# Mixture-of-experts stage of a two-block model: the smallest group's experts two at a time in plain fp32

## What is computed

```python
def moe_ffn(x, w_router, router_bias, w_gate, w_up, w_down):     # 256 tokens, D = 1024
    scores = jax.nn.sigmoid(jnp.dot(xt, w_router))
    biased = (scores + router_bias).reshape(N, N_GROUPS, EXPERTS_PER_GROUP)   # 4 groups of 4 experts
    group_score = jnp.sum(lax.top_k(biased, TOP_K)[0], axis=-1)
    g_sel = jnp.argmax(group_score, axis=-1)                     # each token picks ONE group
    ...                                                          # and two experts of it
    h = jax.nn.silu(jnp.einsum('nd,edf->enf', xt, w_gate)) * jnp.einsum('nd,edf->enf', xt, w_up)
    h = h * gates.T[:, :, None]                                  # 16 experts, hidden width 256
    y = jnp.einsum('enf,efd->nd', h, w_down)
```

## Time and profile before

| what | value |
|---|---|
| median of 3 runs | 1137.94 us (1137.85 to 1139.21) |
| time of the profiled execution | 1140.78 us |
| its span | 1138.8 us |
| granted TensorE clock | 0.995 of full speed |
| TensorE matmul busy | 1109.2 us, 97% |
| VectorE busy | 796.6 us, 70% |
| ScalarE busy | 587.5 us, 52% |
| HBM read | 212.63 MB |

### The profile page before, as it was taken

The page is one execution under the profiler, slowest core; times in us unless marked ns, Lnnn a source line. Parts: engine busy times, 40 slices in busy tenths (PEclk is TensorE's granted clock), DMA queues, the critical chain, the costliest instruction groups (busy, mean ns, idle before and its releaser), DMA issues.

```text
span 1138.8 us, 17173 instructions
## 1 busy us (share of the span) xinstructions
PE 1109.2 (97%) x6740; PEld 968.9 (85%) x6740; DVE 796.6 (70%) x1012; ACT 587.5 (52%) x744; POOL 109.1 (10%) x191
## 2 busy tenths in 40 slices
PE   9999999999999999999999999999899999999996
PEld 8999989999788888899787888878797878887885
DVE  5445634687576666659868668996779777578986
ACT  5344455664544344455733456775247624457761
POOL 3000020100000000046300000000156000000000
PEclk9999999999999999999899999999999999999999
DMA  9764444555365555534113969995334119789960
GB/s 297 225 182 126 131 142 147 152 184 182 101 235 184 184 187 192 173 121 149 38 58 105 333 229 322 348 367 199 103 112 148 38 40 294 260 268 350 361 240 38
DMA packets 164983, 214.72 MB, mean 189 GB/s; under 512 B 9778, under 2 KB 145098, under 8 KB 164912
## 3 DMA queue, kind: packets, MB, share of 16 engines
q1 hardware_dynamic: 162288, 209.37, 56.2%
q0 software_dynamic: 1312, 3.88, 1.1%
q10 hardware_dynamic: 1312, 0.49, 0.2%
HBM read 212.63 MB, written 1.09 MB: 188 GB/s over the span
## 4 chain that ended last, share of the span: by engine, by line
PE 84%; DVE 11%; ACT 3%; issue 2%; POOL 0%; ACTq 0%; DVEq 0%
PE ps L863 18%; PE ps L864 18%; PE ps L865 18%; PE ps L1002 7%; PE ps L1001 3%; PE ps L966 3%; PE ps L901 2%; PE ps L899 2%; PE ps L900 2%; DVE wlo L1923 2%; PE ps L940 2%; PE ps L932 2%; PE ps L951 2%; DVE arena L2269 1%; PE ps L924 1%
## 5 line engine op out<-in xcount | busy, mean ns | idle before, releaser
L1923 DVE TENSOR_TENSOR wlo<-raw,whi 128x2048 fp32r<-128x2048 f32 (+3 forms) x157 | 337.6, 2155 | 152.6 <-ACT whi L1531 150.9
L1531 ACT ACTIVATE whi<-raw 128x2048 fp32r<-128x2048 f32 (+3 forms) x157 | 280.9, 1794 | 123.5 <-PE ps L1002 61.5
L863 PE MATMUL ps<-whi,act_both 128*128 128x256 f32 (+2 forms) x464 | 146.2, 315 | 2.8 <-DVE act_both L1940 2.5
L864 PE MATMUL ps<-wlo,act_both 128*128 128x256 f32 (+2 forms) x464 | 144.8, 312 | 0.0
L865 PE MATMUL ps<-whi,act_both 128*128 128x256 f32 (+2 forms) x464 | 144.7, 312 | 0.0
L1923 DVE TENSOR_TENSOR wlo<-arena,whi 128x2048 fp32r<-128x2048 f32 (+1 forms) x48 | 107.9, 2248 | 35.1 <-ACT whi L1531 33.8
L1002 PE MATMUL ps<-act_both,whi 128*128 128x512 f32 x344 | 119.1, 396 | 0.6 <-DVE wlo L1923 0.6
L863 PE MATMUL ps<-act_both,whi 128*128 128x256 f32 x408 | 117.4, 288 | 0.0
L865 PE MATMUL ps<-act_both,wlo 128*128 128x256 f32 x408 | 115.4, 283 | 0.0
L864 PE MATMUL ps<-act_both,whi 128*128 128x256 f32 x408 | 115.4, 283 | 0.0
L1531 ACT ACTIVATE whi<-arena 128x2048 fp32r<-128x2048 f32 (+1 forms) x48 | 90.4, 1884 | 26.5 <-PE ps L865 26.5
(11 more groups left out here) (311 smaller groups left out, 2134.8 us busy)
## 6 DMA issues: line engine op xcount, KB each, us to landing
raw<-in_w_in SPq DMA_DIRECT2D x45, 1024.0 KB, 5.5
raw<-in_w_down SPq DMA_DIRECT2D x27, 1024.0 KB, 5.4
raw<-in_w_gu SPq DMA_DIRECT2D x22, 1024.0 KB, 5.1
arena<-in_w_gate SPq DMA_DIRECT2D x32, 512.0 KB, 5.5
arena<-in_w_up SPq DMA_DIRECT2D x32, 512.0 KB, 7.0
raw<-in_w_gate SPq DMA_DIRECT2D x28, 512.0 KB, 5.2
raw<-in_w_up SPq DMA_DIRECT2D x28, 512.0 KB, 6.6
arena<-in_w_down SPq DMA_DIRECT2D x14, 1024.0 KB, 6.0
```

The source lines that it names most:

```text
L863: pe.matmul(o, ah, bh, start=first, stop=False)
L864: pe.matmul(o, ah, bl, start=False, stop=False)
L1531: act.activation(whi[:, c % 3, 0:n], raw_of(c, v)[:, 0:n], ACT.Copy).then_inc(hi_made, 1)
L1923: dve.tensor_tensor(wlo[:, c % 3, 0:n], raw_of(c, v)[:, 0:n], whi[:, c % 3, 0:n].bitcast(F32), ALU.subtract)\
```

## The change

1. The groups are ranked by size (a VectorE sort of size and number, L2540 to L2548 of the new file). The largest is wide as before, the second and third have 128 slots each, the smallest has 64.
2. The smallest group's four experts leave `MOE_SEQ` and the split rings. They run as two pairs in plain fp32 on the raw tiles. The 64 rows are the stationary operand, once for each half of the array's columns, and expert b of the pair writes PSUM partitions 64b to 64b+63. Tiles P (gate and up of both experts, two blocks of D, 1 MB, four per pair) and Q (down, one half of D, 1 MB, two per pair) hold four matmuls of 512 columns each. They use the same ring of six slots, which they free when TensorE has used them (`pair_used`).
3. P tiles stand behind A4, D1, B4, A5, D2, B5, A6, B6; Q tiles behind D8, B10, D9, B11. The hidden rows of a pair are transposed once for both experts (`turn_pair`).
4. `GU_BANKS` has two banks instead of three; the third is the pairs'.
5. The loops of ScalarE and VectorE go by tile number n: what follows tile n-3 on TensorE is done around the split of tile n. The gather writes 320 columns instead of 384.

```diff
-MOE_SEQ = [0, 1, 2, 4, 5, 6, 7, 8, 9, 10, 11, 12, 13, 14, 15, 3]
+MOE_SEQ = [0, 1, 2, 4, 5, 6, 7, 8, 9, 10, 11, 3]
-GU_BANKS = (0, 1, 3)
+GU_BANKS = (0, 1)
+PAIR_BANK = 3
+PAIR_IN_AFTER = {("A", 4): (0, 0), ("D", 1): (0, 1), ("B", 4): (0, 2), ("A", 5): (0, 3),
+                 ("D", 2): (1, 0), ("B", 5): (1, 1), ("A", 6): (1, 2), ("B", 6): (1, 3)}
+PAIR_OUT_AFTER = {("D", 8): (0, 0), ("B", 10): (0, 1), ("D", 9): (1, 0), ("B", 11): (1, 1)}
+PAIR_TURN_AT = (4, 6)
...
+            def room(i):
+                pair, n = raw_user(i)
+                if pair:
+                    sp.wait_ge(pair_used, n + 1)
+                elif n >= 0:
+                    sp.wait_ge(hi_made, n + 1)
+                    sp.wait_ge(lo_made, n + 1)
...
+                def pair_in(x, i):
+                    n = pair_tile(l, "P", x, i)
+                    room(PAIR_AT[n])
+                    for b in range(2):
+                        for j, w in enumerate(w_gate_up):
+                            d = raw_pair(n)[:, (2 * b + j) * 512:(2 * b + j + 1) * 512].rearrange("p (k c) -> p k c", k=2)
+                            sp.dma_start(d, w[row(12 + 2 * x + b)][:, 2 * i:2 * i + 2, :]).then_inc(raw_in[pair_slot(n)], 16)
...
-                            if kind == "A" and part == 0 and j >= 3:
-                                pe.wait_ge(m_prod, l * 20 + j - 2)
-                            o = ps[:, GU_BANKS[j % 3], :].rearrange("p (a b) -> p a b", a=2)
+                            if kind == "A" and part == 0 and j >= 2:
+                                pe.wait_ge(m_prod, l * 16 + j - 1)
+                            o = ps[:, GU_BANKS[j % 2], :].rearrange("p (a b) -> p a b", a=2)
...
+                def pair_gate_up(x, i):
+                    n = pair_tile(l, "P", x, i)
+                    pe.wait_ge(raw_in[pair_slot(n)], landed_at(PAIR_AT[n]))
+                    if x and i == 0:
+                        pe.wait_ge(pair_prod, l * 2 + x)
+                    w = raw_pair(n).rearrange("p (e two k c) -> p e two k c", e=2, two=2, k=2)
+                    for kk in range(2):
+                        k = 2 * i + kk
+                        for b in range(2):
+                            z = pe.matmul(ps[64 * b:64 * b + 64, PAIR_BANK, :].rearrange("p (a c) -> p a c", a=2),
+                                          xg_pairs[:, k, :], w[:, b, :, kk, :], start=k == 0, stop=k == KD - 1)
+                    z.then_inc(pair_used, 1)
...
                 def gathered(k):
                     dve.wait_ge(xg_h, l * KD + k + 1)
-                    dve.tensor_tensor(xg_lo[:, k, :], ps[:, k, 0:SLOTS], xg_hi[:, k, :].bitcast(F32), ALU.subtract).then_inc(xg_l, 1)
+                    dve.tensor_copy(xg_pairs[:, k, :], ps[:, k, 2 * P:2 * P + 64])
+                    dve.tensor_tensor(xg_lo[:, k, 0:2 * P], ps[:, k, 0:2 * P], xg_hi[:, k, 0:2 * P].bitcast(F32), ALU.subtract).then_inc(xg_l, 1)
...
-                split("A", MOE_SEQ[1])
-                for p in range(1, N_EXP):
-                    product(p - 1)
-                    split("B", MOE_SEQ[p])
...
+                for n in range(FIRST_LOOP, len(MOE_ORDER) + 3):
+                    kind, e, part = MOE_ORDER[n - 3]
+                    if kind == "B" and part == parts_of("B", e) - 1:
+                        product(MOE_SEQ.index(e))
+                    if n < len(MOE_ORDER):
+                        split_lo(T_L + l * L_TILES + J_MOE + n, 0, TW // parts_of(*MOE_ORDER[n][0:2]))
```

More of the change, by code:

```diff
@@ L91, in run_ends, with split_tiles @@
 def run_ends(p):
[L93 to L106, removed]
+    return p == N_RUN - 1 or run_begins(p + 1)
+FLUSH = [p for p in range(N_RUN - 1) if wide(MOE_SEQ[p]) and run_ends(p)]
+GROUP_END = [p for p in range(N_RUN) if not wide(MOE_SEQ[p]) and run_ends(p)]
+PUT_READ = min(p for p in range(N_RUN) if MOE_SEQ[p] // 4 == 2)
 def moe_order():
-    at = {}
+    order, turned, paired, pair_in = [], {}, {}, {}
+    def split_tiles():
+        return sum(kind in "ABD" for kind, e, part in order)
     def add(kind, e):
-        for part in range(parts_of(kind, e)):
-            at[kind, e, part] = len(at)
-    for p in range(N_EXP):
+        order.extend((kind, e, part) for part in range(parts_of(kind, e)))
+        if (kind, e) in PAIR_IN_AFTER:
+            order.append(("P",) + PAIR_IN_AFTER[kind, e])
+            if order[-1][2] == 3:
+                pair_in[split_tiles() - 1] = order[-1][1]
+        if (kind, e) in PAIR_OUT_AFTER:
+            order.append(("Q",) + PAIR_OUT_AFTER[kind, e])
+    for p in range(N_RUN):
         add("A", MOE_SEQ[p])
@@ L137, in moe_used, with pair_tile, raw_sequence, add @@
     return moe_tile(l, kind, e, parts_of(kind, e) - 1) + 1
-def moe_at(n):
-    return (n - T_L) % L_TILES - J_MOE if n >= T_L else -1
+def pair_tile(l, kind, x, i):
+    return l * len(PAIR_ORDER) + PAIR_ORDER.index((kind, x, i))
+def raw_sequence():
+    at, pair_at = {}, {}
+    seq = []
+    def add(slot, transfers, table, n):
+        table[n] = len(seq)
+        seq.append((slot, transfers, table is pair_at, n))
+    for n in range(T_L):
+        add(n % 3, 1, at, n)
+    for l in range(LAYERS):
+        for j in range(J_MOE):
+            n = T_L + l * L_TILES + j
+            add(n % 3, 1, at, n)
+        for i, (kind, e, part) in enumerate(RAW_ORDER):
+            if kind in "PQ":
+                add(i % RAW, 4 if kind == "P" else 2, pair_at, pair_tile(l, kind, e, part))
+            else:
+                add(i % RAW, 1 if kind == "D" else 2, at, moe_tile(l, kind, e, part))
+    return seq, at, pair_at
+J_UQ, J_UKV, J_WO, J_RT, J_MOE = 6, 8, 10, 14, 15
+RAW_SEQ, RAW_AT, PAIR_AT = raw_sequence()
+def landed_at(i):
+    return 16 * sum(transfers for slot, transfers, pair, n in RAW_SEQ[:i + 1] if slot == RAW_SEQ[i][0])
+def raw_user(i):
+    users = [entry for entry in RAW_SEQ[:i] if entry[0] == RAW_SEQ[i][0]]
+    return users[-1][2:] if users else (False, -1)
 def raw_slot(n):
-    return moe_at(n) % RAW if moe_at(n) >= 0 else n % 3
+    return RAW_SEQ[RAW_AT[n]][0]
 def landed(n):
[L152 to L162, removed]
+    return landed_at(RAW_AT[n])
+def pair_slot(n):
+    return RAW_SEQ[PAIR_AT[n]][0]
 L_COLS = [4, 5, 6, 7, 0, 1, 2, 3]
@@ L213, in shape_constants @@
     c[:, C_UP:C_UP + P] = np.arange(P)[:, None] < np.arange(P)[None, :]
[L214 removed]
+    slot = np.arange(SLOTS)
+    c[:, C_SLOT:C_SLOT + SLOTS] = S + np.where(slot < 2 * P + 64, slot, slot - 64)
     dist = S - 1 - np.arange(2 * S)
@@ L1445, in down @@
                             pair = q if wide(e) else GROUP_BANK[e // 4 - 1]
-                            if first and part == 0:
-                                bank_free(p, pair)
+                            if first and part == 0 and not wide(e):
+                                bank_flushed(pair)
                             for half in range(part, 2 // parts + part):
@@ L1455, in down, with scatter @@
                         x.then_inc(tile_used, 1)
-                def scatter(t, half, q0, q1):
-                    for q in range(q0, q1):
+                def scatter(t, half, groups):
+                    for q in groups:
                             w = put_t[:, q, t * P:(t + 1) * P]
```

269 lines of the change are left out of this document (169 added, 100 removed).

## The result

The changed kernel takes 1145.3 us (median of five runs, 1143.39 to 1149.48) against 1137.94: 1.0067 times as long, 95% interval 1.0051 to 1.0082. It is slower; the forecast was 1127 and the range ended at 1143. The profiled execution took 1149.48 us, 8.7 more than the profiled one of before; it is the slowest of the five, so what its trace shows is a little worse than the median.

A forecast was written before the change was run, and what follows sets the result against it. TensorE, its matmuls busy 97% of the span, was taken as the bound. Terms of -34.3 + 24.4 + 0.4 - 0.5 + 3.2 + 1.2 gave -5.6 us a layer, -11.2 for two: 1127 us, range 1116 to 1143.

The forecast's parts named there:

- the pair transposes: Two more pairs of transposes on TensorE cost 0.4 us a layer; the pair's Silu, product and copy cost nothing.
- the term of the transfers: Same 48 MB in less time, queue held back from B8 on; 1.2 us a layer lost by A3.
- a sign of being wrong: The prediction is wrong if the queue, held by `pair_used`, starves TensorE already between A6 and B8.
- the landing time of 1 MB: A 1 MB transfer lands 6.3 us after its issue, 5.2 us where the queue runs dry.
- the 1.2 us at A3: Late weights and a product behind D10's split delay A3; 1.2 us a layer lost.
- the price of a column half: In pair tiles, 512-column passes of 0.43 us run side by side in two halves; 2.03 us a tile.
- rivals 2 and 3: Column halves overlap only in part: about 1138 us, chance 0.13; or don't run side by side: 1166 us, chance 0.14.
- The two banks' wait: A1 waits for expert 0's first product, starting at 642.9 instead of 639.69; 3.2 us a layer lost.
- The gather: 32 matmuls 320 instead of 384 columns wide, two small VectorE operations more; together -0.5 us a layer.
- Rival 4: Transfers become the bound: rate falls to 345 GB/s, some 30 tiles cost 4.5 us a layer; 1136 us, chance 0.10.
- The estimate of partial overlap: Two column halves gain 1.6 times, so a pair tile takes 2.5 us and no gain is left.

The follow-up runs named there:

- e1: The changed kernel with Silu and product of a pair ahead of the next tile's split instead of behind it; 1148.46 us.
- e11: The changed kernel with only the pair transposes one A tile later and their copy ahead of the split; 1142.75 us.
- e5: The changed kernel with pair operations and expert 0's product ahead of splits, pair transposes one A tile later, their copy ahead of the split; 1126.13 us.
- e9: The changed kernel with both experts' gate and up matmuls in one column half, the second expert's own values left out; 1163.62 us.
- e4: The changed kernel with the loops over experts (column halves) and K slices swapped within a P tile; 1144.48 us.

## Why the prediction was wrong

**The step that failed** is the one on the pair transposes: "The Silu, product and copy of a pair are small operations behind splits whose tiles aren't needed yet; nothing." That the tiles aren't needed yet is true, and beside the point: P(1,0) needs the small operation, whatever it stands behind, and stood 4.97 and 6.56 us for it. e1, e11 and e5 together show the price. Under it lies a second slip, in the term of the transfers: it let `pair_used` hold the queue back from B8 on, but the first two P tiles held it already (8.0 and 5.1 us without an issue). The prediction named a place nearby as a sign of being wrong ("if the queue, held back by `pair_used`, starves TensorE already between A6 and B8"), but worked out only when tiles arrive for TensorE, not when they arrive for ScalarE and VectorE, which take their work in order. It also took the landing time of 1 MB from one row of its DMA view, 6.3 us. In the same view of before stands:

```profile
raw<-in_w_down SPq DMA_DIRECT2D x3, 1024.0 KB, 7.1
```

**What it cost**, against the sum. The way from A0 to A3 was forecast at 149.1 - 5.1 = 144.0 us a layer, 288.1 in all (the gather lies ahead of A0), and is 307.8, 19.7 more:

- the stalls at P(1,0), 4.97 + 6.56 = 11.5 us;
- the low clock behind them, 2.6 + 2.0 us: the tile takes 3.61 instead of 1.87 us in both layers, the transposes and B5 behind it the rest;
- two waits at or near a transposition, 1.80 and 0.24 us in each layer, 4.1 us: the same fault in the small, an operation behind a split;
- A1: 43.5 us from A0 to A4 against 39.5 before, 4.0 a layer instead of 3.2, 1.5 us more. The wait itself was forecast too long (2.58), the low clock behind it not at all;
- against that, P and Q tiles are a little cheaper (1.87 and 0.1 for the next product's slower start, 1.97 instead of 2.03: -1.4), and the 1.2 us at A3 did not come, -2.4; that the stall gave the loads time to catch up is likely, and not shown.

That makes 17.9 of 19.7; 1.8 us are not placed.

**Right**: the price of a column half, and with it that rivals 2 and 3 are out (1.87 us, e9). The two banks' wait, its place and its releaser. That the transfers fill the DMA behind the stall: 363 GB/s. The gather: A0 started 0.45 us earlier relative to before in the profiled pair of runs, though the hop of 3 to 4 us makes that no proof. The sum without the misjudged waits: 99.4 us from A4 to A3 with the measured tiles, and e5 has 101.8, of which 0.93 and 0.45 us are waits. That e5 takes 1126.13 and the forecast was 1127 is luck in part: e5 has lost the wait at A1 as well, for which the sum held 3.2 us a layer. Without it the sum gives 281.7 us from A0 to A3 in both layers, and e5 has 283.2; the rest of the agreement lies in the stretches that hop.

**Rival 4** had the right cause (`pair_used` holds loads back) with the wrong mechanism and price: not a lower rate over thirty tiles, but two loads, A6's and D4's, that came late and whose lateness an in-order engine passed on.

**The estimate of partial overlap** that stood apart from the sum was worked out from the figure for three column tiles in the Trainium skill, TensorE: Matmul & The Clock Gate, Measured speedup vs the span model (1.6 times, 2.5 us a tile). It does not hold for two halves of 64 columns in plain fp32 here: 3.57 / 1.87 = 1.9 times.

## What to carry to other kernels

When work is put into an in-order engine behind an operation that waits for a transfer, ask who waits for the small work, not who waits for the operation ahead of it. A stall that is taken away at one operation may stand at the next one behind the same late transfers; take away all of them before judging the idea (e1 alone would have buried a change that is worth about 1%). And tiles that are held until TensorE reads them shorten the lead of a ring for every load behind them, here while the DMA still had time free (0.54 in the first hold).

## Not expected of the hardware

- Two plain fp32 blocks of 64 stationary columns run side by side in 1.87 us, 3.57 us in the same half, and the order of the four matmuls in the program makes no difference (1.87 us in e4).
- A wait of 2.58 us of TensorE was enough to lose 1.6 us more at a lower granted clock (0.65 on average from 641 to 645), while 1.80 us at 738.67 left it at 1.00. In e4's first layer a wait of 2.57 us at the same place cost no clock: A0 to A4 took 667.23 - 625.35 = 41.9 us there and 43.5 in its second layer. e9's first layer and e11's second are like that, too (41.9 us each). So what a short wait costs differs from layer to layer and run to run.
